# Modulation and key/value weight tiles laid out as whole rows, key/value tiles split two tiles ahead, and evictions that wait for their time

## The reference, cut to what matters

```python
shift, scale, gate = jnp.split(silu_c @ w_ada[l] + b_ada[l], 3, axis=-1)
shift_c, scale_c, gate_c = jnp.split(silu_cc @ w_ada[l] + b_ada[l], 3, axis=-1)
h = _modulate(_rmsnorm(xs, norm_g[l]), shift[:, None], scale[:, None])
hc = _modulate(_rmsnorm(cs, norm_g[l]), shift_c, scale_c)
pc_kv = hc @ w_l[:, OFF_K:OFF_ZA]
...
p = h @ w_l
q = _rope(_rmsnorm(_heads(p, OFF_Q, N_Q_HEADS), q_norm_g[l]), cos, sin) * q_scale
k = _rope(_rmsnorm(_heads(p, OFF_K, N_KV_HEADS), k_norm_g[l]), cos, sin)
```

## Time and profile before

| | |
|---|---|
| median of 3 runs | 2819.8 us (2818.88 to 2822.88) |
| the profiled execution, its own time | 2815.83 us |
| its span | 2814.0 us |
| TensorE busy | 2772.6 us (99%) |
| VectorE, ScalarE, GpSimd busy | 2093.6, 1484.3, 347.6 us |
| mean granted TensorE clock | 0.996 of full speed |
| HBM read | 612.69 MB |

### The profile page before, as it was taken

How to read it: one execution, slowest core, us unless ns; L and a number is a source line. 1 busy time by engine, 2 the same in 40 slices (tenths; PEclk the granted TensorE clock), 3 DMA queues, 4 the chain that set the end, 5 groups by cost and what they waited for, 6 DMA issues and landing times. The chain is left out here.

```text
span 2814.0 us, 43494 instructions
## 1 busy us (share of the span) xinstructions
PE 2772.6 (99%) x16296; PEld 2401.5 (85%) x16296; DVE 2093.6 (74%) x3615; ACT 1484.3 (53%) x2430; POOL 347.6 (12%) x1005
## 2 busy tenths in 40 slices
PE   7999999999999999999999999999999999999999
PEld 4678888888888888888888888888888888888888
DVE  3368877888988878787877877888888865566654
ACT  3355544555566666666666644545454544444443
POOL 0003410000002252423233210000000000000000
PEclk8999999999999999999999999999999999999999
DMA  8966657888966555555555578788768756655554
GB/s 279 320 222 217 217 193 258 289 263 290 313 181 208 175 167 175 177 179 177 174 176 173 168 263 283 255 289 297 247 214 279 259 183 186 196 190 189 187 183 148
DMA packets 217587, 621.85 MB, mean 221 GB/s; under 512 B 20240, under 2 KB 73632, under 8 KB 216608
## 3 DMA queue, kind: packets, MB, share of 16 engines
q1 hardware_dynamic: 217376, 619.08, 67.5%
HBM read 612.69 MB, written 4.21 MB: 219 GB/s over the span
## 5 line engine op out<-in xcount | busy, mean ns | idle before, releaser
L268 PE MATMUL ps<-act,whi 128*128 128x512 f32 (+1 forms) x6560 | 1760.3, 399 | 17.6 <-ACT whi L244 10.5
L253 DVE TENSOR_TENSOR wlo<-raw,whi 128x1024 fp32r<-128x1024 f32 (+3 forms) x883 | 1045.1, 1189 | 451.0 <-ACT whi L244 250.1
L268 PEld LDWEIGHTS ps<-act,whi 128*128 128x128 f32 (+1 forms) x6560 | 1168.7, 189 | 226.3 <-issue 16.0
L268 PE MATMUL ps<-act,wlo 128*128 128x256 f32 (+2 forms) x6416 | 995.0, 288 | 3.6 <-DVE wlo L253 3.6
L244 ACT ACTIVATE whi<-raw 128x1024 fp32r<-128x1024 f32 (+3 forms) x883 | 880.6, 1024 | 204.8 <-PE ps L268 149.8
L268 PEld LDWEIGHTS ps<-act,wlo 128*128 128x128 f32 (+1 forms) x6416 | 896.5, 190 | 74.4 <-DVE wlo L253 6.8
L244 ACT ACTIVATE t<-ps 128x256 f32<-128x256 f32 (+2 forms) x400 | 149.9, 376 | 460.3 <-PE ps L268 408.7
L263 DVE SCALAR_TENSOR_TENSOR acc<-raw,c_act,acc 128x1024 f32<-128x1024 f32 x210 | 267.8, 1277 | 0.0
L259 POOL TENSOR_SCALAR small<-small 128x2 f32<-128x2 f32 (+3 forms) x256 | 94.4, 369 | 991.9 <-DVE small L259 972.1
L253 POOL TENSOR_TENSOR small<-small 128x2 f32<-128x2 f32 (+2 forms) x460 | 171.2, 372 | 258.0 <-ACT t L244 172.4
L244 ACT ACTIVATE t<-t 128x256 f32<-128x256 f32 (+3 forms) x248 | 108.0, 438 | 176.3 <-DVE t L253 152.8
(11 more groups left out here) (224 smaller groups left out, 1972.2 us busy)
## 6 DMA issues: line engine op xcount, KB each, us to landing
raw<-in_w SPq DMA_DIRECT2D x425, 512.0 KB, 4.9
raw<-in_w_mod SPq DMA_DIRECT2D x192, 512.0 KB, 4.7
raw<-in_w_ada SPq DMA_DIRECT2D x96, 512.0 KB, 6.3
raw<-in_w_gate SPq DMA_DIRECT2D x88, 512.0 KB, 4.7
raw<-in_w_up SPq DMA_DIRECT2D x88, 512.0 KB, 4.7
raw<-in_w_out SPq DMA_DIRECT2D x64, 512.0 KB, 5.7
raw<-in_w_down SPq DMA_DIRECT2D x64, 448.0 KB, 3.7
raw<-in_p_a SPq DMA_DIRECT2D x32, 512.0 KB, 5.7
```

The lines of the kernel that those rows point to most:

```text
L253: return (q or DV).put(lambda e: e.tensor_tensor(o, a, b, op), needs, cost=max(0.4, size(o) * 0.0036) if q else 0.07 + size(o) * 0.00104)
L268: return PE.put(lambda e: e.matmul(o, w, x, start=start, stop=stop), needs, tell, cost)
```

## The change

Layout: `_lay_out` now builds `w_s`, one contiguous 128 x 1024 block for each scale/shift tile, and `w_kv`, one for each key/value tile; `w_ada` keeps only the gate columns (4096 and up). The loads of these tiles read whole rows. Order: a key/value item in the list now only loads and splits (its "pe" stores the split's tokens); the matmuls are an `X` item two `S` tiles (`S_LATE`) later. `S_PLACE` moves to match, and the piece of three units comes ahead of that of four. `load_k1` moves behind group 8's key/value loads. Evictions: `k_job` and `v_job` call `hop` before their first copies.

```diff
-S_PLACE = [(1, 3), (2, 7)] + [(j, p) for j in range(3, 9) for p in (4, 7)]
+S_PLACE = [(2, 0), (2, 5)] + [(j, p) for j in range(3, 9) for p in (2, 5)]
+S_LATE = 2
...
     def k_job(kv, bank, tok):
         sq, f = yield from t2.take()
+        yield from hop(tok + f)
         t = act(sq[:, :], bank[:, :], ACT.Square, tok + f)
         kg, f = yield from t2.take()
+        yield from hop(f)
         c = copy(kg[:, :], bank[:, :], f + tok, scale=col(C_KG))
...
     def v_job(kv, bank, tok):
         vt, f = yield from t2.take()
+        yield from hop(tok + f)
         c = copy(vt[:, :], bank[:, :], tok + f)
...
     def s_group(j):
-        k, n = GROUPS[j]
-        c, m = 128 * n, 8 // n
-        return [{"kind": "S", "src": w_ada[:, kt:kt + m, off:off + c], "shape": m, "cols": 1024, "pe": s_pe, "sec": sec, "j": j,
-                 "kts": range(kt, kt + m)} for sec, off in ((0, 2048 + 128 * k), (1, 128 * k)) for kt in range(0, 16, m)]
...
+        return [{"kind": "S", "src": src["w_s"][i], "cols": 1024, "pe": s_pe, "sec": sec, "j": j, "kts": range(kt, kt + m)}
+                for i, (j_, sec, kt, m) in enumerate(_s_tiles()) if j_ == j]
...
+    k_group_pieces = deque({"kind": "B", "src": src["w_kv"][i, :, 0:128 * m * n], "cols": 128 * m * n, "pe": run_group,
+                            "units": units[u:u + m], "kts": range(k, k + n)} for i, (u, m, k, n) in enumerate(_kv_tiles()))
+    landed = deque()
+
+    def run_landed():
+        landed.popleft()()
+
+    def load_piece():
+
+        it = k_group_pieces.popleft()
+        landed.append(lambda: run_group(it))
+        add({**it, "pe": lambda new: it.update(new)})
+
+    s_tiles = [(x, (j, i) in S_PLACE) for j in range(len(GROUPS)) for i, x in enumerate(s_group(j))]
+    for n, (x, loads) in enumerate(s_tiles):
+        add(x)
+        if loads:
+            load_piece()
+        if n >= S_LATE and s_tiles[n - S_LATE][1]:
+            add({"kind": "X", "run": run_landed})
+    while k_group_pieces:
+        load_piece()
+    for n in range(16 - sum(x for _, x in s_tiles[:-S_LATE])):
+        add({"kind": "X", "run": run_landed})
     add({"kind": "L", "run": load_k1})
...
+def _s_tiles():
+
+    return [(j, sec, kt, 8 // n) for j, (k, n) in enumerate(GROUPS) for sec in range(2) for kt in range(0, 16, 8 // n)]
+
+
+def _kv_tiles():
+
+    return [(u, m, k, n) for k, n in GROUPS for u, m in ([(0, 7)] if n == 1 else [(0, 3), (3, 4)])]
```

More of the change, by code:

```diff
@@ L30 @@
 LOADS = 8
+GROUPS = [(0, 1), (1, 1)] + [(k, 2) for k in range(2, 16, 2)]
 C_C, C_CC, C_C2, C_BADA, C_NG, C_FG, C_BMOD, C_N1, C_N2 = 0, 16, 32, 48, 96, 112, 128, 224, 240
@@ L552, in run_gemm, with together @@
             u.after(u.bank, last)
-    def together(units, weights, groups=((0, 4), (4, 4), (8, 4), (12, 4)), parts=None, **more):
+    def together(units, weights, **more):
         units = [Unit(*u) for u in units]
         out = []
[L559 to L563, removed]
+        for k in range(0, 16, 4):
+            out.append([{"kind": "B", "src": weights(i, 2, slice(128 * k, 128 * k + 512)), "shape": 2, "cols": 1024,
+                         "pe": run_group, "units": units[i:i + 2], "kts": range(k, k + 4), **more}
+                        for i in range(0, len(units), 2)])
         return out
@@ L698, in act_c @@
         t1.give(big, toks)
-    GROUPS = [(0, 1), (1, 1)] + [(k, 2) for k in range(2, 16, 2)]
     def s_pe(it):
@@ L1205, in m_items @@
     def m_items():
-        secs = [(M_GATE, 0, C_BADA + 32, lambda kt, h: src["w_ada"][128 * kt:128 * kt + 128, 4096 + 1024 * h:5120 + 1024 * h])]
+        secs = [(M_GATE, 0, C_BADA + 32, lambda kt, h: src["w_ada"][128 * kt:128 * kt + 128, 1024 * h:1024 + 1024 * h])]
         for s in (1, 0, 2, 4, 3, 5):
@@ L1246, in block_kernel @@
     start(norm_in())
-    w_ada = src["w_ada"].rearrange("(k p) n -> p k n", p=128)
     def s_group(j):
-        k, n = GROUPS[j]
-        c, m = 128 * n, 8 // n
-        return [{"kind": "S", "src": w_ada[:, kt:kt + m, off:off + c], "shape": m, "cols": 1024, "pe": s_pe, "sec": sec, "j": j,
-                 "kts": range(kt, kt + m)} for sec, off in ((0, 2048 + 128 * k), (1, 128 * k)) for kt in range(0, 16, m)]
[L1255 to L1265, removed]
+        return [{"kind": "S", "src": src["w_s"][i], "cols": 1024, "pe": s_pe, "sec": sec, "j": j, "kts": range(kt, kt + m)}
+                for i, (j_, sec, kt, m) in enumerate(_s_tiles()) if j_ == j]
+    units = [Unit(512, rhs_both, lambda b, t, i=i: start((k_job if i < 4 else v_job)(i % 4, b, t))) for i in range(KV_FIRST)]
+    k_group_pieces = deque({"kind": "B", "src": src["w_kv"][i, :, 0:128 * m * n], "cols": 128 * m * n, "pe": run_group,
[18 more added lines that the diff above has]
+        add({"kind": "X", "run": run_landed})
     add({"kind": "L", "run": load_k1})
-    stream.extend(k_group_pieces)
     HALVES = (8, 8)
@@ L2145, in _lay_out @@
     d["a_log"], d["dt_bias"] = x["a_log_2"], x["dt_bias_2"]
-    d["w_ada"] = x["w_ada"][0]
+    ada = x["w_ada"][0].reshape(16, 128, 6144)
+    d["w_s"] = np.stack([ada[kt:kt + m, :, c:c + 128 * GROUPS[j][1]].transpose(1, 0, 2).reshape(128, 1024)
+                         for j, sec, kt, m in _s_tiles() for c in (2048 * (1 - sec) + 128 * GROUPS[j][0],)])
+    d["w_kv"] = np.zeros((len(_kv_tiles()), 128, 1024), np.float32)
+    for i, (u, m, k, n) in enumerate(_kv_tiles()):
+        d["w_kv"][i, :, 0:128 * m * n] = d["w1"][12 + u:12 + u + m, :, 128 * k:128 * k + 128 * n].transpose(1, 0, 2).reshape(128, -1)
+    d["w_ada"] = np.ascontiguousarray(x["w_ada"][0][:, 4096:])
     d["w_mod"] = x["w_mod_2"][0]
```

## The result

The changed kernel takes **2792.3 us** (median of 4 runs, 2791.32 to 2793.06); the kernel before, run beside it, 2821.3. The ratio is 0.9903, 95% interval 0.9889 to 0.9917, or 27.4 us of 2820 (23 to 31). Between the two profiled executions the spans differ by 22.7 us, 2814.0 to 2791.3, where the sum said 19.0.

A forecast was written before the change was run, and what follows sets the result against it. TensorE was taken as the bound, busy 2772.6 of 2814.0 us, with early waits from late splits and loads. Terms 11.1 - 0.5 + 4.7 + 2.2 + 1.5 = 19.0 gave 2796.8, on medians 2800.8 us; range 2793 to 2813.

The forecast's parts named there:

- The head, 11.1: From 25.25 to 62.13 us, the start of group 3: gain of 11.1 us, bounds 5 and 13.
- no hole in the loads at 42 to 46 us: Sign that the forecast holds: in the head, the loads go on without a gap from 42 to 46 us.
- Group 3, -0.5: From 62.13 to 76.77 us: loss of 0.5 us, as the first piece's split can be late; bounds -2 and 0.
- Groups 4 to 7, 4.7: 76.77 to 142.28 us: groups fall from 16.38 to 15.2, gain 4.7; loads need 13.0 plus a 2.5 us refill each.
- the loop of late splits and blocked loads: First 200 us: TensorE waits on a late split, SP waits for its seven raw tiles (84.2 us), loads come late again.
- Rival C: TensorE never waits for a load; four groups gain 7.0 us, whole kernel 2794 us; chance 0.15.
- Group 8, 2.2: From 142.28 to 160.52 us: a 0.89 us wait goes and a 1.4 us unit moves; gain 2.2, bounds 0.5 and 3.
- Evictions, 1.5 up to 200 us, then 0: Key stage: 2.98 us split wait goes, new 1.5 us wait before v7; net gain 1.5, bounds -4 and +3.
- From the mark on, 0: After 200 us, through the attention stage to the end: costed at nothing, bounds -3 and +1.
- Rivals D: Slower: ScalarE's queue in the key stage becomes the bound, 26.6 us lost, 2829 us; chance 0.03.
- E: No net change: head start given back where group 8 and v7 meet, within 5.6 us of 2820; chance 0.05.
- One sign of being wrong: The forecast is wrong if TensorE's waits after 140 us add up to more than 6 us.

The follow-up runs named there:

- late_1: The changed kernel with key/value pieces loaded and split one tile ahead instead of two; ratio to the kernel before 0.9903 (0.9888 to 0.9918).
- block_1k: The changed kernel with its contiguous 512 KB scale/shift blocks stored as four planes of 128 rows of 1 KB; ratio to the kernel before 0.9917.

## Why the prediction was right, and where it was not

*The head, 11.1.* Measured 9.4 (62.13 to 52.74). The steps came in their order, 1.2 to 2.3 us late: tile 7 at 31.0 for 29.8, tile (2,0) at 32.25 for 31.1, group 0's piece at about 37.7 for 35.4. The 3.8 us that one lone tile took to land were too little here: the two loads issued at 26.16 us have a median of 5.2. Then TensorE's small tiles ran at half clock (1.08 us for what took 0.64), and the column flips of group 1 (1.02 us) stand ahead of the last of them; I had priced neither. The piece itself, the end of the dead time and full clock in group 1's piece came out (6.81 for 7.18; 8.23 for 2.4 + 6.0). "Meanwhile the loads go on" did not: there is still a hole in the loads, and the sign "no hole in the loads at 42 to 46 us" failed:

```profile
43.00:46.00 3.00, 3.00 (x35) 1.88 (x37) 0.03 (x1) 0.00 (x0) 0.00 (x0) 1.00 0.06 20
```

It cost TensorE nothing at once, since the next five tiles were already in.

*Group 3, -0.5.* Measured -1.1, but the wait in it is a load of 0.87 us, not the split that I named.

*Groups 4 to 7, 4.7.* Measured 6.6, inside the bounds (0 to 7.0). **This is the step that failed in its reason**: "the loads need 13.0 and, because SP is held up once in each long piece, one refill". No refill is seen: the four groups are TensorE's, three of 14.64 to 14.66 us and one of 14.96. And the rows alone, which in that step are what brings 16.38 down, bring nothing; 4.0 of the 6.6 come with the order alone, the tile's lead over its split. I had named the loop of late splits and blocked loads and then costed it by the loads alone. Rival C, which had TensorE never wait for a load in these groups, was right about them, and with 2794 came nearest to the time.

*Group 8, 2.2.* Measured 2.8 (18.27 to 15.48): the wait of 0.89 and the unit ahead of the last tile went as worked out.

*Evictions, 1.5 up to 200 us, then 0.* Measured 3.3 to the mark. The wait of 2.98 went and the new one ahead of v7 came, at 1.26 for 1.5 predicted. The difference is a term that the sum lacked: behind the old wait, which ends at 196.93, the granted clock was 0.66 on the mean up to 202.0 us, 1.7 us lost (0.34 of 5.07):

```profile
196.93:202.00 5.07, 5.07 (x22) 4.47 (x23) 5.04 (x5) 3.12 (x5) 0.00 (x0) 0.66 0.52 158
```

With rows and order the same is seen, larger: waits of 3.15 and 1.41 us and the 2.9 behind the first, less the 1.26 ahead of v7, are 6.2 of the 6.1 measured.

*From the mark on, 0.* 1.75 measured, not of the change's making as far as the traces tell (last section).

So 9.4 - 1.1 + 6.6 + 2.8 + 3.3 + 1.75 = 22.75, the spans' 22.7. Of the 3.7 us by which it exceeds the sum, 1.75 are that last term, 1.9 the groups, 1.8 the evictions and 0.6 group 8, less 1.7 in the head and 0.6 in group 3. With the spans' 22.7 the time would have been 2797.1, inside the range. The medians differ by more, 29.0: the profiled execution of before, at 2815.8, was faster than all four runs of it beside the change, and the step that carried a gain from that execution over to the medians took for granted that the change would leave their distance as it was. It was 4.0 before; after, the profiled execution (2793.06) lies 0.7 above its median.

Rivals D and E: nothing like them is in the trace; the waits after 145 us on splits add up to 1.7. One sign of being wrong did come by its letter: all of TensorE's waits after 140 us add up to 7.4 us, where more than 6 was to show an error. It was set too low: 4.8 of them come after the mark and are no waits on splits, and the kernel before has 4.9 of the same (12.1 in all).

## What to carry to other kernels

A DMA share of 0.98 doesn't say that the loads set the pace: ask which wait ends last, and whether faster loads alone would move it (here they did not: 65.51 to 65.36 us in four groups). It was the 1.06 and 1.22 us of splitting a tile that is used as it lands, and one tile of lead hid them, after which, and in these groups only then, longer rows paid. When a wait of TensorE is priced, the slow clock that may follow it is to be priced too, from the trace's own clock rows, as a range and not as a certainty.

## What the runs showed that I had not expected

**The same wait is not always followed by the slow clock.** Far behind the change TensorE waits 2.2 us for an operand in both kernels. Before, and then after:

```profile
1974.65 0.47 PE L268 MATMUL ps<-act,whi 128*128 128x512 f32 x1 [2.19 <-DVE act L263]
1974.96 1.23 PE L268 MATMUL ps<-act,wlo 128*128 128x256 f32 x8
1975.99 3.50 PE L268 MATMUL ps<-act,whi 128*128 128x512 f32 x8
```

```profile
1953.48 0.47 PE L271 MATMUL ps<-act,whi 128*128 128x512 f32 x1 [2.18 <-DVE act L266]
1953.79 1.11 PE L271 MATMUL ps<-act,wlo 128*128 128x256 f32 x8
1954.73 2.00 PE L271 MATMUL ps<-act,whi 128*128 128x512 f32 x8
```

Eight matmuls take 3.50 us in one and 2.00 in the other. In the table above the stretch from the mark to the end is 2099 us with the slow piece and 2097.3 without it, in kernels with and without each part. Of the thirteen traces of this case nine have the slow piece, late_1 and block_1k among them, which have all three parts. In the key stage it was the same: a wait of 3.15 us and one of 2.21 us were each followed by the slow clock in one kernel and not in another. Each kernel was traced once, so that this is scatter between executions is argued from the pattern and not shown. Taken so, it is 1.7 us that no edit here controls, and one profiled execution can't price a change finer than that.

**Parts of a stage repeat to a hundredth, and can agree by chance.** From group 8's piece to the mark, the two kernels with new order and yielding evictions take 546.95 and 546.96 us, with the same waits, though their rows differ. Stages cut at matching instructions resolve what whole times, whose intervals here are some 3 to 5 us on either side, can't. But the old order with yielding evictions takes 546.97 by other means: it has no wait ahead of v7 (1.26 us in the changed kernel) and has the slow clock at its start, 1.7 us, in its place. Waits and granted clock of a stage are to be read beside its length.
